# A decoder trunk whose weight blocks GpSimd splits: the high part of a block rounded whole instead of by halves

## What is computed

```python
for layer in range(DEPTH):                      # DEPTH = 2
    h = h + 0.5 * swiglu(rmsnorm(h, ffn1_norm), w_gate, w_up, w_down)       # 1024 -> 2816 -> 1024
    hn = rmsnorm(h, mix_norm[layer])
    if layer % 2 == 0: mix = concat([gla_mixer(..), s5_mixer(..)]) @ ev_w_out
    else:              mix = dsa_mixer(hn, od_w_in, od_w_out, ...)          # selected sparse attention
    h = h + mix
    h = h + cross_attn(rmsnorm(h, xa_norm), mem_n, xa_wq, xa_wk, xa_wv, xa_wo)   # 256 memory tokens
    h = h + 0.5 * swiglu(rmsnorm(h, ffn2_norm), w_gate, w_up, w_down)
return rmsnorm(h, final_norm)
```

## Time and profile before

| | |
|---|---|
| median of 3 runs | 2291.08 us (2280.89 to 2292.57) |
| profiled execution, its own time | 2290.61 us |
| its span, first to last instruction | 2288.8 us |
| TensorE matmuls busy | 2219.7 us, 97% |
| VectorE busy | 1031.3 us, 45% |
| ScalarE busy | 454.4 us, 20% |
| GpSimd busy | 1522.7 us, 67% |
| weights read | 203.48 MB through one queue, 27.2% of the DMA engines' time |
| granted TensorE clock, mean | 0.984 of full speed |

### The profile page before, as it was taken

The page is one execution under the profiler, slowest core; times in us unless marked ns, Lnnn a source line. Parts: engine busy times, 40 slices in busy tenths (PEclk is TensorE's granted clock), DMA queues, the critical chain, the costliest instruction groups (busy, mean ns, idle before and its releaser), DMA issues.

```text
span 2288.8 us, 30161 instructions
## 1 busy us (share of the span) xinstructions
PE 2219.7 (97%) x10546; PEld 1814.0 (79%) x10546; DVE 1031.3 (45%) x1290; ACT 454.4 (20%) x796; POOL 1522.7 (67%) x1528
## 2 busy tenths in 40 slices
PE   8999999999999999999999999998899999999997
PEld 6788888878886888887888888886777868888885
DVE  6575595674333332234343233364882333322334
ACT  2211112033113211101221111142253132111111
POOL 6677787545872776676776677774655637666764
PEclk9999999999999999999999999999999999999998
DMA  5233223222331232232332232331222212222222
GB/s 184 78 115 115 96 97 121 84 70 79 111 106 38 94 99 96 96 101 92 106 97 96 96 96 97 97 97 65 83 84 70 88 42 97 96 96 96 97 97 78
DMA packets 114165, 214.10 MB, mean 94 GB/s; under 512 B 12688, under 2 KB 13216, under 8 KB 113696
## 3 DMA queue, kind: packets, MB, share of 16 engines
q1 hardware_dynamic: 110736, 203.48, 27.2%
q10 hardware_dynamic: 3344, 9.52, 1.2%
HBM read 208.76 MB, written 4.19 MB: 93 GB/s over the span
## 4 chain that ended last, share of the span: by engine, by line
PE 93%; DVE 5%; ACT 1%; issue 1%; DMA 0%; POOL 0%; SPq 0%; DVEq 0%; ACTq 0%
PE ps L363 28%; PE ps L365 28%; PE ps L364 28%; PE ps L895 1%; PE ps L920 1%; PE ps L876 1%; DVE arena L2036 1%; DVE col L2035 1%; PE ps L633 0%; PE ps L809 0%; PE ps L377 0%; PE ps L516 0%; PE ps L843 0%; PE ps L862 0%; PE ps L627 0%
## 5 line engine op out<-in xcount | busy, mean ns | idle before, releaser
L363 PE MATMUL ps<-x,w_split 128*128 128x512 f32 (+1 forms) x2872 | 1119.6, 390 | 19.5 <-POOL w_split L347 10.4
L365 PE MATMUL ps<-x,w_split 128*128 128x512 f32 (+1 forms) x2872 | 1108.6, 386 | 0.0
L364 PE MATMUL ps<-x,w_split 128*128 128x512 f32 (+1 forms) x2872 | 1108.6, 386 | 0.0
L347 POOL TENSOR_TENSOR w_split<-w_raw,w_split 128x512 fp32r<-128x512 f32 x762 | 1027.2, 1348 | 63.6
L343 POOL TENSOR_SCALAR w_split<-w_raw 128x512 fp32r<-128x512 f32 x762 | 499.5, 655 | 677.1 <-PE ps L365 667.7
L363 PEld LDWEIGHTS ps<-x,w_split 128*128 128x128 f32 x2872 | 543.9, 189 | 140.8 <-issue 20.1
L364 PEld LDWEIGHTS ps<-x,w_split 128*128 128x128 f32 x2872 | 544.3, 190 | 108.6 <-issue 2.9
L365 PEld LDWEIGHTS ps<-x,w_split 128*128 128x128 f32 x2872 | 543.7, 189 | 108.5
L1528 DVE TENSOR_TENSOR tu<-ps,rstd 128x512 f32<-128x512 f32 x88 | 60.7, 690 | 337.9 <-PE ps L365 337.9
L1565 DVE TENSOR_TENSOR x<-arena,x 128x512 fp32r<-128x512 f32 x88 | 115.8, 1329 | 203.4 <-ACT x L1100 203.4
L1052 ACT ACTIVATE sg<-tg 128x512 f32<-128x512 f32 x88 | 55.6, 632 | 707.6 <-DVE tg L1525 706.0
(11 more groups left out here) (264 smaller groups left out, 1335.1 us busy)
## 6 DMA issues: line engine op xcount, KB each, us to landing
w_raw<-in_stream SPq DMA_DIRECT2D x762, 256.0 KB, 2.5
s_tables<-kv ACTq DMA_DIRECT2D x4, 512.0 KB, 3.3
arena<-s_tables ACTq DMA_DIRECT2D x4, 512.0 KB, 5.2
out<-h ACTq DMA_DIRECT2D x8, 256.0 KB, 2.2
h<-in_xT SPq DMA_DIRECT2D x1, 1536.0 KB, 8.7
arena<-in_memT SPq DMA_DIRECT2D x1, 1024.0 KB, 10.2
arena<-in_memT ACTq DMA_DIRECT2D x1, 1024.0 KB, 4.8
h<-in_xT SPq DMA_DIRECT2D x1, 512.0 KB, 3.9
```

The lines of the kernel that those rows point to most:

```text
L347: pool.tensor_tensor(W[:, s, 1, c], raw[:, s, c], W[:, s, 0, c].bitcast(F32), ALU.subtract).then_inc(split_ready if half else S("half_spli ...
L363: pe.matmul(dst, wh, xh, start=start, stop=False)
L364: pe.matmul(dst, wh, xl, start=False, stop=False)
L365: return pe.matmul(dst, wl, xh, start=False, stop=stop)
```

## The change

GpSimd's loop is written anew. Blocks in the eight pairs are split as before (`split`, now with the count for its semaphore as an argument). Every other block, 365 of them, goes through `split_whole`: it waits for both halves of the load and for `block_done >= b - 1`, rounds all 1024 columns in one `tensor_scalar`, and then does the two subtractions by halves, each with the same signal as before. The wait for `half_done` is gone for these blocks. SyncE, TensorE and the other engines are unchanged.

```diff
-            def split(b, half):
+            def split(b, half, count):
...
-                pool.wait_ge(S(f"w_hi{'ab'[half]}"), b + 1)
+                pool.wait_ge(S(f"w_hi{'ab'[half]}"), count)
...
-            b = 0
-            while b < N_BLOCKS:
-                n = 2 if b in PAIRS else 1
+            def split_whole(b):
+
+                s = b % 2
                 for half in range(2):
-                    for e in range(n):
-                        split(b + e, half)
-                b += n
+                    pool.wait_ge(S(f"raw{s}{'ab'[half]}"), 16 * (b // 2 + 1))
+                pool.wait_ge(S("block_done"), b - 1)
+                pool.tensor_scalar(W[:, s, 0, :], raw[:, s, :], 1.0, 0.0, ALU.mult, ALU.add).then_inc(S("w_hi"), 1)
+                pool.wait_ge(S("w_hi"), whole.index(b) + 1)
+                for half in range(2):
+                    c = slice(half * HALF, (half + 1) * HALF)
+
+                    pool.tensor_tensor(W[:, s, 1, c], raw[:, s, c], W[:, s, 0, c].bitcast(F32), ALU.subtract
+                                       ).then_inc(split_ready if half else S("half_split"), 1)
+
+            paired = [b + e for b in sorted(PAIRS) for e in range(2)]
+            whole = [b for b in range(N_BLOCKS) if b not in paired]
+            for b in range(N_BLOCKS):
+                if b in whole:
+                    split_whole(b)
+                elif b in PAIRS:
+                    for half in range(2):
+                        for e in range(2):
+                            split(b + e, half, paired.index(b + e) + 1)
```

## The result

The changed kernel takes 2319.7 us (median of 4 runs, 2315.78 to 2322.15) against 2288.57 us of the kernel before beside it (4 runs, 2280.89 to 2292.57). The ratio is 1.0139, with a 95% interval of 1.0117 to 1.0160: slower by 31 us. The profiled execution took 2315.78 us, its span 2314.0 us; between the two profiled spans lie 25.2 us. TensorE's mean granted clock is 0.985, beside 0.984 before.

A forecast was written before the change was run, and what follows sets the result against it. The prediction took TensorE's matmuls to bound the kernel, with GpSimd's lead at stake. Its terms, 12.6 + 0.9 + 11.8 + 3.0 = 28.3 us on 2290.61, gave 2319 us, range 2308 to 2327.

The forecast's parts named there:

- the twelve places named: Seven pair ends, an eighth, and four feed-forward ends: matmuls wait for GpSimd about 1.8, 0.9 and 2.9 us.
- The lead in the steady stream: Over 300 blocks: some 2.6 us of GpSimd's lead over TensorE remain, cost 0.
- The rounding: GpSimd's rounding of 1024 columns: taken as 1.14 us, between bounds of 0.62 and 1.24.
- six steps: Key/value tiles alternating with output tiles, 590 to 650 us: six delays of 0.5 us each, 3.0 in all.
- Pair ends: Block after a pair: TensorE stalls 1.80 us at seven of eight pairs, 12.6 in all, and 0.91 at the eighth.
- Feed-forward ends: Last two blocks of each of four down projections: stall of 2.94 us each, 11.8 in all.
- late only if a load takes over 3.8: DMA queue: the second half, loaded in 2.5 us, is there in time, cost 0, unless a load exceeds 3.8 us.
- The pair that follows: cost 0.: Pair behind each feed-forward's last two blocks: still waits for half_done as before, cost 0.
- Key/value tiles: Where 256-column key/value tiles alternate with output tiles, 590 to 650 us: 0.5 us late six times, 3.0 in all.
- A shift stays whole: After a pair: the next limit, the fifth tile's bank, is free early, so the 1.80 us shift is not given back.
- B: Rival: more blocking and late loads at 26 places, up to 0.8 us more each, 21 us, giving 2340; chance 0.12.
- C: Rival: VectorE relieved, shortening chains TensorE waits for in attention and memory stretches, some 20 us, giving 2299; chance 0.06.

The follow-up runs named there:

- e7_and_chains: Changed kernel with blocks behind pairs, each down projection's last two, 92-108, 160-175 and 264-291 by halves again, 288 whole: 2292.3 us, ratio 1.0012.
- e5_round_twice_last: Changed kernel with the last block of each down projection rounded twice, one rounding behind the other: 2322.79 us in a single run.
- e3_both: Changed kernel with the eight blocks behind pairs and the last block of each down projection by halves again: 2297.85 us, ratio 1.0039.

## Why the prediction was right

The predicted 2319 us stands against 2319.7, inside the range of 2308 to 2327, and the mechanism is the one forecast: TensorE waits at the twelve places named, and the blocks there start later by nearly what was reckoned. That the two times agree to 0.7 us is luck. The kernel before measured 2288.57 beside the change, 2.0 us under the 2290.61 that the sum starts from, and the change cost 31.1 us by the medians, 2.8 more than the 28.3 forecast. The terms were not all right either.

- **The lead in the steady stream.** Held: the median lead of all whole blocks in the changed kernel is 2.36 us, most lie between 2.0 and 2.7. No wait there, and rounding whole in 288 blocks costs 0.2 to 5.5 us.
- **The rounding.** Taken 1.14 us from a memset's fixed part, measured 1.05 where undisturbed and 1.08 in the mean. The prediction's estimate from the Trainium skill (GPSIMD Engine Reference, Performance versus the Vector engine), 1.06, was nearer. With it the sum would have been smaller by 18 x 0.08 = 1.4 us (twelve places and six steps), not 1.3.
- **Pair ends.** Forecast 1.80 each and 0.91; the waits shift the block by 1.75 to 1.81 and 0.87. But 0.32 us come back within the block: in the kernel before, the first matmul behind the sum of squares lasts 0.79 and the next starts 0.63 later; after the wait they start 0.31 apart. Net 1.44, so the two terms are 10.7 together, not 13.5.
- **Feed-forward ends.** Forecast 4 x 2.94 = 11.8; measured 2.79 three times and 3.45 once, 11.8. The first is longer because a load came late (GpSimd waits for it 2.43 us, until 374.44). The prediction's "late only if a load takes over 3.8" was right as a condition; the median of the earlier trace rows hid that a load issued at 364 took 6.8 us in the kernel before too. So the term came out whole partly by luck: three stalls were 0.15 shorter and one 0.5 longer than forecast.
- **"The pair that follows: cost 0."** Held for GpSimd; wrong for TensorE's clock, which halved behind two of the four stalls: some 3.2 us that no step had.
- **Key/value tiles.** Forecast 3.0 as six steps of 0.5, measured 2.5: four steps of 0.40 us and one of 0.84 at block 95, where the prediction had counted nothing. Going back to halves there removed them. The sum of a step was right, but not the operation that pays: the rounding was not held up (1.06 us), the first subtraction was, with 1.6 us of the 2.85 that the two take here in place of 2.5:

```profile
612.84 1.06 POOL L356 TENSOR_SCALAR w_split<-w_raw 128x1024 fp32r<-128x1024 f32 x1 [1.08 <-PE ps L381]
613.98 2.85 POOL L361 TENSOR_TENSOR w_split<-w_raw,w_split 128x512 fp32r<-128x512 f32 x2
```

- **Absorption.** "A shift stays whole" held for the stalls. The 1.3 us given back at blocks 79 and 80 are clock: TensorE waits 4.21 us there in both kernels, but then runs 6.8 us at half the clock (from 494) where it ran 10.2 in the kernel before (from 486). What else looked like absorption, 1.45 us at 740 and at 1890 us, is a half-clock stretch that the kernel before has there (from 708, behind a wait of 2.22 us) and the changed one has not, behind a wait of 2.45:

```profile
704.00:712.00 8.00, 5.78 (x23) 4.61 (x22) 2.00 (x3) 1.16 (x2) 3.01 (x3) 0.79 0.20 66
```

That is the window in the kernel before, with the granted clock at 0.79 in the mean; the same window of the changed kernel has 1.00:

```profile
714.00:722.00 8.00, 5.55 (x29) 4.45 (x28) 2.99 (x4) 1.09 (x2) 4.39 (x3) 1.00 0.31 96
```

- **The rivals.** B, blocking and late loads, is real but small: one late load, and VectorE's chain ahead of block 173, 0.45 us in the changed kernel and up to 1.7 in its variants. C, VectorE's relief, is refuted as a gain: with 66 us less of busy time no kernel became faster.

The sum for the spans was 28.3 against 25.2 in the profiled pair; the medians of the runs lie 31.1 apart. The difference of 6 us comes from which executions were profiled: the one of the kernel before was 2.0 us above its median, that of the changed kernel (2315.78, the fastest of its four) 3.9 us under. Why single executions differ stays open: the runs scatter by 6 to 12 us. That the half-clock stretches, which fall differently in each, make the scatter would fit, but isn't shown.

No version tried is faster than the kernel before. The nearest, e7_and_chains, is level with it within a few tenths of a per cent.

## What to carry to other kernels

Where the bound engine waits for nobody, a helper's saving is worth nothing and its lead everything: before fusing two small operations, ask which wait the fused one must inherit (here the later of two), and look for the places where less than one unit of work lies between that release and the need. In this kernel they are the seams, pairs and ends of stages, and twelve of 365 blocks held some 70% of the cost. Two things help to price them: the row in which the later release already stands (its start plus the new operations gives the new time directly), and a look at single loads and at the clock behind each new stall, not at medians.

## What the runs showed of the hardware that was not expected

- A stall of TensorE of 2.2 to 3.3 us was followed, at 8 of 12 places, by 3.4 us at the granted clock 0.50, which cost about 1.6 us; stalls up to 1.2 us by none in the changed kernel, those of 3.8 us and more by one at 4 of 4 (e5_round_twice_last, a single execution). So a stall of 2.8 us could cost half as much again as it lasted.
- A GpSimd rounding of 128 x 1024 took 1.05 us against 0.62 for 128 x 512: 0.43 us for 512 more columns, and by a straight line through these two 0.19 fixed (an estimate).
- VectorE's two-input instructions got shorter over the whole kernel when GpSimd issued fewer and longer operations (L1534 with 1424 ns in the mean before is L1550 with 926 after), but single ones got longer: in e3_both three of them, beside two subtractions in a row, took 4.93 us in place of 3.41, and the three before them 2.87. That the missing rounding between the subtractions is the cause is not shown. That the whole splits beside this chain are the cause is: with halves there, e7_and_chains waits 2.7 us again in place of 4.4.
